# Delta-rule solver: inverses of the 16x16 diagonal blocks on VectorE, TensorE from size 16 on, and the next key projection ahead of the solver

## What is computed

```python
    decay = jnp.exp(jnp.where(lower_incl, gcum[..., :, None] - gcum[..., None, :], -jnp.inf))
    kb = kc * bc[..., None]
    l_mat = jnp.where(strict, jnp.einsum('nbhid,nbhjd->nbhij', kb, kc) * decay, 0.0)
    rhs = jnp.concatenate([vc * bc[..., None], kb * jnp.exp(gcum)[..., None]], axis=-1)
    sol = lax.linalg.triangular_solve(l_mat, rhs, left_side=True, lower=True, unit_diagonal=True)
    ...
    def step(s, xs):
        q_d, k_d, u_c, w_c, a_c, d_c = xs
        v_new = u_c - jnp.einsum('bhcd,bhde->bhce', w_c, s)
        o = jnp.einsum('bhcd,bhde->bhce', q_d, s) + jnp.einsum('bhij,bhje->bhie', a_c, v_new)
        s = s * d_c[..., None, None] + jnp.einsum('bhcd,bhce->bhde', k_d, v_new)
        return s, o
```

## Time and profile before

| what | us |
|---|---|
| median of the three runs | 1915.28 |
| lowest and highest of them | 1913.55, 1915.35 |
| span of the profiled execution, first to last instruction | 1911.3 |
| total time of the profiled execution | not listed apart |
| PE, DVE, ACT, POOL busy in it | 1860.4, 1257.7, 976.3, 525.6 |
| delta stage, head 0 to the last product of head 7 | 809.0 to 1306 |

### The profile page before, as it was taken

One profiled execution on the slowest core, in us unless ns is written; L12 is line 12 of the kernel. 1 busy time (PEld: TensorE's weight loads), 2 busy tenths in 40 slices (PEclk: granted clock), 3 DMA queues, 4 the chain that ended last, 5 costly groups with the idle time before them and its releaser, 6 DMA issues.

```text
span 1911.3 us, 32275 instructions
## 1 busy us (share of the span) xinstructions
PE 1860.4 (97%) x11917; PEld 1737.8 (91%) x11917; DVE 1257.7 (66%) x2099; ACT 976.3 (51%) x1869; POOL 525.6 (28%) x398
## 2 busy tenths in 40 slices
PE   8899999999998999999999999999999999999997
PEld 5899999999997799999999999997888989899897
DVE  7758787778666765467666766676333577366476
ACT  6534242424457655557555755574223576365463
POOL 0714141323100200255355534550000034142330
PEclk9999999999999999999999999999999999999999
DMA  8143335553423420011101111111333403223232
GB/s 332 62 132 122 122 116 165 179 180 119 145 76 111 120 61 1 23 39 61 50 33 38 60 49 33 38 45 56 99 99 105 149 23 113 87 89 118 82 133 67
DMA packets 52241, 178.36 MB, mean 93 GB/s; under 512 B 6820, under 2 KB 10020, under 8 KB 51888
## 3 DMA queue, kind: packets, MB, share of 16 engines
q1 hardware_dynamic: 48864, 162.46, 25.1%
q0 software_dynamic: 3280, 14.60, 2.4%
HBM read 170.17 MB, written 4.24 MB: 91 GB/s over the span
## 4 chain that ended last, share of the span: by engine, by line
PE 75%; DVE 9%; ACT 8%; issue 5%; POOL 2%; DMA 1%; SPq 0%; ACTq 0%; DVEq 0%; POOLq 0%
PE ps L2621 50%; PE ps L2832 14%; PE ps L2625 4%; PE ps L2919 2%; PE ps L3152 1%; DMA raw<-W 1%; PE ps L3076 1%; ACT e_hi L1261 1%; DVE e_lo L2024 1%; ACT ps L1246 1%; DVE d_os L2515 1%; DVE d_c L2383 1%; PE ps L3106 1%; PE ps L3208 1%; DVE ps L2066 1%
## 5 line engine op out<-in xcount | busy, mean ns | idle before, releaser
L2621 PE MATMUL ps<-h_hi,w_hi 128*128 128x384 f32 (+2 forms) x720 | 241.1, 373 | 8.0 <-DVE h_lo L1800 4.0
L2621 PE MATMUL ps<-h_lo,w_hi 128*128 128x384 f32 (+2 forms) x720 | 236.9, 361 | 0.0
L2621 PE MATMUL ps<-h_hi,w_lo 128*128 128x384 f32 (+2 forms) x720 | 228.0, 356 | 0.0
L1730 DVE TENSOR_TENSOR w_lo<-raw,w_hi 128x1024 fp32r<-128x1024 f32 (+1 forms) x98 | 122.8, 1253 | 129.8 <-ACT w_hi L933 129.8
L933 ACT ACTIVATE w_hi<-raw 128x1024 fp32r<-128x1024 f32 (+1 forms) x98 | 102.9, 1050 | 153.9 <-PE ps L2621 151.9
L2621 PEld LDWEIGHTS ps<-h_hi,w_hi 128*128 128x128 f32 x720 | 130.1, 188 | 28.7 <-DVE h_lo L1800 8.2
L2621 PEld LDWEIGHTS ps<-h_hi,w_lo 128*128 128x128 f32 x720 | 133.0, 188 | 13.5
L2621 PEld LDWEIGHTS ps<-h_lo,w_hi 128*128 128x128 f32 x720 | 133.1, 188 | 13.0 <-issue 1.2
L2621 PE MATMUL ps<-g_hi,w_hi 128*128 128x384 f32 (+2 forms) x444 | 132.9, 346 | 0.8 <-DVE w_lo L1730 0.5
L2621 PE MATMUL ps<-g_lo,w_hi 128*128 128x384 f32 (+2 forms) x444 | 131.8, 343 | 0.0
L2621 PE MATMUL ps<-g_hi,w_lo 128*128 128x384 f32 (+2 forms) x444 | 131.7, 343 | 0.0
(11 more groups left out here) (465 smaller groups left out, 5459.7 us busy)
## 6 DMA issues: line engine op xcount, KB each, us to landing
raw<-W SPq DMA_DIRECT2D x221, 512.0 KB, 3.6
w_mod<-WMOD SPq DMA_DIRECT2D x68, 512.0 KB, 3.8
g_row<-g_rows POOLq DMA_DIRECT2D x8, 768.0 KB, 4.5
X<-XT SPq DMA_DIRECT2D x4, 768.0 KB, 6.9
a_sw<-i_n POOLq DMA_DIRECT2D x40, 64.0 KB, 1.9
w_first<-WMOD SPq DMA_DIRECT2D x4, 512.0 KB, 10.9
X<-XT SPq DMA_DIRECT2D x1, 2048.0 KB, 14.0
x_spill<-X POOLq DMA_DIRECT2D x1, 2048.0 KB, 9.5
```

Of the source, the lines that this page charges most:

```text
L1730: v.tensor_tensor(lo, src, hi.bitcast(F32), ALU.subtract).then_inc(s("w_split"), 1)
L2621: return pe.matmul(out, lhsT, rhs, start=start, stop=stop)
```

## The change

The solver's first four levels (sizes 1 to 8) are replaced. DVE's six products now carry the minus sign and a reciprocal of its own (`k_neg`), SP writes the six matrices to DRAM and reads the 48 diagonal 16x16 blocks back so that each lies in one partition (`d_b`, with a row of padding per matrix that makes the stride regular). DVE inverts all 48 at once, in place, in 14 steps of two products and two sums on up to 56 elements (`inverse_step`). SP returns the blocks in six small DMAs (`d_xc`), and DVE spreads each over its row of blocks with a mask (`own_block`). PE goes on from size 16: 9 groups and three levels. The key projection of the next head stands ahead of the solver (45 of its 48 pieces), the value projection fills the scan; the norm of a head's output moves to the top of the next head. POOL's list is in another order, and the pairs of semaphores in the attention that told of a step and its successor are one each. In the last head the second gate projection of the merge stands ahead of the solver.

```diff
-LEVELS = 7
+SUB = 16
+NB = P // SUB
+LV0, LEVELS = 4, 7
...
+            def blocks_out(h):
+
+                sp.wait_ge(s("d_l"), h + 1)
+                sp.dma_start(DL[:, 0:P].rearrange("c p j -> p c j"), d_l[:, 0]).then_inc(s("d_blocks"), 16)
+                sp.wait_ge(s("d_blocks"), h * 32 + 16)
+                sp.dma_start(d_b[0:NB * NCH], diagonal).then_inc(s("d_blocks"), 16)
+
+            def blocks_back(h):
+
+                sp.wait_ge(s("inv_a"), 28 * h + 28)
+                for c in range(NCH):
+                    sp.dma_start(d_xc[:, c], d_b[NB * c:NB * c + NB]).then_inc(s(f"d_xin{c // 2}"), 16)
+
+            load_groups(B_LAST1 + 2 * RING, W_HEAD)
+            with sp.Fori(0, H, 1) as h:
+                blocks_out(h)
+                load(h * 4 + W_HEAD, W_HEAD % RING)
+                load(h * 4 + (W_HEAD + 1), (W_HEAD + 1) % RING)
+                blocks_back(h)
+                load(h * 4 + (W_HEAD + 2), (W_HEAD + 2) % RING)
+                load(h * 4 + (W_HEAD + 3), (W_HEAD + 3) % RING)
...
-                g.wait_ge(s("t_first"), h * 3 + 3)
-                for lv in (1, 2):
-                    for gr in range(3):
-                        level(lv, 2 * gr, 2 * gr + 2)
...
+                g.wait_ge(s("d_l"), h + 1)
+                level(LV0)
+                level(LV0 + 1)
+                next_low(5)
+                if not first:
+                    g.wait_ge(s("od_ss"), h)
+                g.wait_ge(s("d_tokc"), h * 2 + 1)
+                g.wait_ge(s("hc"), h * 2 + 2)
                 keys(0)
                 keys(1)
-                g.wait_ge(s("lvl"), h * 10 + 10)
+                if not final:
+                    g.wait_ge(s("d_diff"), h * 2 + 2)
+                    g.wait_ge(s("d_qe"), h * 2 + 2)
+                    rows_load(h + 1)
+                queries(0)
+                queries(1)
+                if not final:
+                    spread(h + 1)
+                g.wait_ge(s("sv_q"), h * 9 + 3)
+                level(LV0 + 2)
...
+                if not first:
+                    out_add(h - 1)
+                split_next(b[4])
+                if not first:
+                    out_low(h - 1)
+                    out_gain(h - 1)
+
+                m = d_b[0:NCH * NB]
+
+                def inverse_step(n):
+
+                    f, r = n + 1, SUB - 2 - n
+                    low = (m[:, f + 1:, f:f + 1], m[:, f:f + 1, 0:f], m[:, f + 1:, 0:f])
+                    up = (m[:, 0:r, r:r + 1], m[:, r:r + 1, r + 1:], m[:, 0:r, r + 1:])
+                    sums = [d_bt[0:NCH * NB, k, 0:f * r].rearrange("p (i j) -> p i j", i=r) for k in range(2)]
+                    for k, (col, row, rest) in enumerate((low, up)):
+                        if n:
+                            v.wait_ge(s("inv_a"), h * 28 + (2 * n - 1 + k))
+                        v.tensor_tensor(sums[k], col.to_broadcast([NCH * NB, r, f]), row.to_broadcast([NCH * NB, r, f]), ALU.mult)\
+                         .then_inc(s("inv_m"), 1)
+                    for k, (col, row, rest) in enumerate((low, up)):
+                        v.wait_ge(s("inv_m"), h * 29 + (2 * n + 2 + k))
+                        v.tensor_tensor(rest, rest, sums[k], ALU.add).then_inc(s("inv_a"), 1)
+
+                v.wait_ge(s("d_blocks"), h * 32 + 32)
+                v.memset(m.rearrange("p i j -> p (i j)")[:, 0:SUB * SUB:SUB + 1], 1.0).then_inc(s("inv_m"), 1)
+                for n in range(SUB - 2):
+                    inverse_step(n)
...
+                if not final:
...
+                    conv(h + 1, 0, b[4])
+                if not first:
+                    out_rows(h - 1)
+                split_next(b[6])
+
+                for gr in range(3):
+                    v.wait_ge(s(f"d_xin{gr}"), h * 32 + 32)
+                    x = d_x[:, 2 * gr:2 * gr + 2].rearrange("p c (b j) -> p c b j", b=NB)
...
+                if final:
+                    query(b[5], 0, KT - 1)
+                else:
+                    piece(b[5], next_key, 6 * KT - 3)
...
-                for i in range(18):
+                for i in range(9):
                     mid(i)
                     if i:
                         grow(i - 1)
```

More of the change, by code:

```diff
@@ L1635, in _ @@
             take(first[1])
-            activate(0, first[1].ahead(2), False)
-            take(Blk(B_DN, 0, 2))
-            with a.Fori(0, H - 1, 1) as h:
-                dn_head(h, False)
-            dn_head(H - 1, True)
+            a.preload_act_table_set(SILU_SET)
+            split(first[1].ahead(2))
+            key_silu(0)
+            dn_head(0, True, False)
+            with a.Fori(1, H - 1, 1) as h:
+                dn_head(h, False, False)
+            dn_head(H - 1, False, True)
             def merged(it):
@@ L3113, in dn_head @@
                 last.then_inc(s("d_kk"), 1)
+                pe.wait_ge(psum_read[b[2].pair], b[2].turn + 2)
+                tokens(0)
+                if not first:
+                    pe.wait_ge(s("od_copy"), h)
+                pe.wait_ge(s("d_silu"), h * 3 + 2)
                 for c in range(NC_X):
@@ L3117, in dn_head @@
                 last.then_inc(s("d_kq"), 1)
[L3118 to L3119 removed]
                 dn_gemm(h, 3)
[L3121 to L3124 removed]
+                query(b[4], 0, 2)
+                if not first:
+                    pe.wait_ge(s("d_tokc"), h * 2 + 1)
+                    out_sum(h - 1)
+                query(b[4], 2, 5)
                 pe.wait_ge(psum_read[b[3].pair], b[3].turn + 2)
@@ L3258, in _, with attended @@
             dn_gemm(0, 2)
-            with pe.Fori(0, H - 1, 1) as h:
-                dn_head(h, False)
-            dn_head(H - 1, True)
-            for j in range(2, 4):
-                merge_gemm(0, j)
+            dn_head(0, True, False)
+            with pe.Fori(1, H - 1, 1) as h:
+                dn_head(h, False, False)
+            dn_head(H - 1, False, True)
+            def attended(k0, k1):
+                blk = Blk(B_MERGE, 0, 2)
+                if k0 == 0:
+                    pe.wait_ge(s("w_split"), blk.w + 1)
+                    pe.wait_ge(psum_read[blk.pair], blk.turn + 1)
+                for k in range(k0, k1):
+                    pe.wait_ge(s("o_split"), k + 1)
+                    for i, (w, x) in enumerate(((w_hi, oat_hi), (w_hi, oat_lo), (w_lo, oat_hi))):
+                        last = mm(bank(blk, 1), w[:, blk.pair, k, :], x[:, k], k == 0 and i == 0, k == KT - 1 and i == 2)
+                if k1 == KT:
+                    last.then_inc(s("gemm_done"), 1)
+            attended(0, 3)
+            out_sum(H - 1)
+            attended(3, KT)
+            merge_gemm(0, 3)
             def merge(it):
```

562 lines of the change are left out of this document (276 added, 286 removed).

## The result

The changed kernel takes **1978.06 us**, the median of four runs (1976.01 to 1979.21), against 1914.41 for the kernel before on the same chip: a ratio of 1.0332, 95% interval 1.0317 to 1.0346. It is slower by 3.3%. The forecast was 1966, with 1885 to 1992 around it.

The account below looks back on a forecast made before the run. PE's work was taken to bound a head; after the change 53.3 us busy plus 17.2 idle made 70.5. Six middle heads at +7 (42) and two end heads at +4 each, together +50 on 1915.28, gave 1966 us, range 1885 to 1992.

Parts of the forecast that it names:

- The deciding term: DVE's all-SBUF inverse takes turns with POOL's queued instructions; it ends at 32.5 us, so PE idles 11.3 us per head.
- the undisturbed walk: Path to the start matrix without POOL's hold-ups: inverse ends at 19.6 us, blocks return in 4.3, matrix at about 23.9.
- DVE's share between two POOL instructions: In each gap between two POOL instructions the inverse gets one or two instructions, 0.8 us in all.
- The blocks: Diagonal blocks written to DRAM in 3.6 us and read back in 3.0, there at 12.6 us into a head.
- PE's idle time ahead of the start matrix: PE arrives at 25.3 us, waits until 36.6 and idles 11.3; 10 to 12 us would show the forecast right.
- the cover: PE's work in a head before its first wait for the solver's start matrix, 22.9 us.
- PE's work in a head: Nine full solver groups of 1.11 us go, 10.0 us, so PE's work falls from 63.3 to 53.3 us.
- The ends: Head 0, without a forerunner's output, and the last head, with nothing filling its scan, cost about +4 us each.
- Rival 1: DVE's inverse isn't held up by POOL: 57 us per head, 1870 us in all; chance 0.20.
- The break-even: Delay of DVE's inverse at which the change neither gains nor loses: 6.6 us, against the 13 expected.
- Rival 2: The inverse ends early, so the spread pair falls behind it: 64.6 us per head, 1922 us; chance 0.10.
- Rival 3: The DRAM path is the bound, 10 us not 6.6: 73 to 75 us per head, some 1990; chance 0.07.

Follow-up runs that it names:

- e1: Changed kernel with POOL's spread pair for the next head moved behind the solver's last mask; 1940.13 us, one run.
- e2: Changed kernel with POOL's key scaling, query scaling and spread pair, and DVE's next-query convolution, moved behind the solver; 1939.98 us, ratio 1.014.
- e3: Changed kernel with the inverse in a free PSUM bank, one input of each product and sum in PSUM, POOL unchanged; 1934.64 us, ratio 1.0103.
- e5: Changed kernel with the edits of e3 and e1 together, the spread pair behind the value scaling; 1890.89 us, ratio 0.987.
- e7: e5 with POOL's first two masks moved behind its query scalings; 1904.44 us, ratio 0.9945.
- e9: Changed kernel with unused PE products (8, 44 and 4) filling PE's three gaps in a head; 1969.55 us, ratio 1.0294.
- e8: e5 with POOL's first masks after the output's gain, row load behind query scalings, value weight split behind the solver's first masks; 1885.47 us, ratio 0.9857.

## Why the prediction was right, and where it was off

**The deciding term held.** The prediction put the inverse's end at 32.5 us and the start matrix at 36.6; they came at 31.6 and 36.1. It had the inverse held up by 12.9 us (19.6 to 32.5); the rows give 12.8. It expected about ten held instructions; there are six, in five pairs. Undisturbed it takes 6.6 us (forecast 7.0), and from its end to the start matrix go 4.5 us (forecast 4.1, where the undisturbed walk has 4.3). e1, e2, e3 and e5 show the cause: move POOL's work or one operand, and the delay goes. Four things stand beside it:

- **DVE's share between two POOL instructions** was taken as one or two instructions a gap, 0.8 us in all. From 1036.0 to 1044.0 DVE got three pairs through in eight microseconds of POOL's work, so the size holds. That the two "strictly take turns" does not: a product was held for 2.67 us over both query scalings, and one in e7 for 4.44 us. Why POOL kept its turn there and not at the key scalings, no run tells. The spread pair still met the inverse, with 2.6 us of undisturbed steps left (forecast 3.2).
- **The blocks** were to be there at 12.6 and were used at 12.1, but this hides two errors. The path through DRAM was sized by the 512 KB loads and a guess, 6.6 us; it took 2.8 us for the write and 2.1 for the read, 4.9, so the blocks lay there at 10.8. DVE came for them only at 12.1, since its two instructions ahead were held by the masks (1.93 and 2.32 us; 0.69 and 0.74 in e7). The estimate of 5.0 us from the Trainium skill ("DMA: Bandwidth & Descriptors", "Anatomy of one DMA"), which the sum did not take, agrees with the 4.9 measured, though the page gives its fit for DMAs issued by GpSimd and these go by SP's queue. The DMA rows:

```profile
d_matrices<-d_l SPq DMA_DIRECT2D x8, 384.0 KB, 2.8
d_xc<-d_b SPq DMA_DIRECT2D x48, 8.0 KB
d_b<-d_matrices SPq DMA_DIRECT2D x8, 48.0 KB, 2.1
```

- **PE's idle time ahead of the start matrix** is 10.3 us in heads 4 to 6, where PE comes at 25.8 (forecast 11.3 and 25.3; the cover is 0.7 us longer than 22.9). In head 3 it is 8.7, outside the 10 to 12 that was to be the sign, because the low clock in the key projection (0.84 us a pair for 0.51) lets PE come 1.6 us later, at 27.4. An idle time is a difference of two arrivals: the matrix came at 36.1 in both, and the head didn't get longer.
- **PE's work in a head** was to be 53.3 us. With the clock up it is 55.0 (e5). The nine full groups went as forecast: from its first product to its last the solver takes 10.6 us in e5 and took 20.5 before. Of the 1.7 us above the forecast 0.7 lies in the cover and the rest behind it. In head 4 of the changed kernel it is 57.4, 2.4 more at the low clock, and in head 3, with the low clock in the key projection, 59.0.

There is luck in the head's 70.5, then. Its busy part was 4.1 us too small (57.4 in head 4 for 53.3) and its idle part 3.1 too large (14.1 for 17.2: 2.2, 10.3, 0.7 and 0.9 for 2.4, 11.3, 2.0 and 1.5), and the two nearly cancel.

**Where the size was off** is the total: +50 us against +63.7. The middle heads were 6 x 7 = 42 and are 6 x 8.0 = 48. What the sum has no term for is the granted clock after the wait: 1.6 us per head, for with the clock up the head takes 70.0 (e9), half a microsecond less than forecast. Behind the start matrix the head took 35.4 us where the forecast had 33.9, and 33.8 with the clock up. The ends were to cost 4 + 4. Head 0 takes 69.9 us where it took 63.1, and head 7 with the step to the merge 64.0 where it took 57.7: 6.8 + 6.3, and some 2 behind them. These two were not walked as the middle head was, and more than half of the missing 13.7 lies there and behind them. No run takes it apart further.

**The rivals.** Rival 1, an inverse that isn't held up, was priced at 57 us per head and 1870 us in all. e3 made exactly that, and the head is 66.7 and the kernel 1934.64. Its price was too low by 65 us, mostly because the walk let DVE's work behind the inverse run undisturbed: 7.7 of the 8.0 us by which the start matrix is late (31.9 for 23.9). In the changed kernel it does, since POOL is through by then; take the inverse out of the way and it meets the same POOL instructions. The break-even given for it (6.6 us of delay) is wrong for the same reason. Rival 2, the spread pair behind the inverse, was priced at 64.6 and 1922; e1 gives 65.9 and 1940. Rival 3, the path through DRAM, is off the critical chain by 1.3 us in a middle head, where DVE never idled for the memset; only in head 0, which has no output norm ahead of it, did it idle 4.2 us.

**What stays open.** Why the clock fell in the key projection in heads 1 to 3 of the changed kernel and not in heads 4 to 6 or in e5, with the same wait of 1.8 us ahead of it, no run tells. Whether more can be had from e8 by a faster return of the blocks wasn't tried.

## What to carry to other kernels

Before a chain of small DVE instructions is put beside POOL's work, look at their operands: with all of them in SBUF each can cost a whole POOL instruction or more, however few elements it has, and a chain of dependent ones pays it each time. One operand in PSUM frees the chain (here 19.4 us became 7.5 for the same work). Then walk every SBUF instruction of DVE up to the one that others wait for against POOL's queue, for a collision that is removed moves to the next of them: only the two edits together made the change a gain, from 1978 to 1891 us with 1915 before.

## What the runs showed of the hardware

- Few elements don't help beside POOL: two products of 12 elements took 2.48 us beside two query scalings (e3), 4.52 beside a query scaling and two masks (e7), and 0.24 alone.
- DVE and POOL don't always alternate: of each of these pairs one product was held over all of POOL's instructions (2.40 and 4.44 us) and the other took under 0.2.
- A DVE instruction with one SBUF tensor and a scalar is held as well: the first tap of a convolution over 770 elements takes 0.62 us at the start of a head and 2.30 beside POOL's mask in the scan of e3:

```profile
1055.85 2.30 DVE L2425 TENSOR_SCALAR d_kc<-d_up,hn 128x770 f32<-128x770 f32 x1
```

- PE's granted clock was 0.50 behind an idle time of 8.6 us and came back some 7 us after PE had begun again. Short waits don't always bring it down: in e8 it was low behind 0.24, 0.84 and 0.90 us in head 3 and stayed up behind 0.23, 1.02 and 0.90 in head 5.
- SP takes 3.91 us to issue the six DMAs that spread 8 partitions over 128, 0.6 us each, where 0.4 had been assumed and the write of the six matrices takes 0.40:

```profile
1028.01 0.40 SPq L728 DMA_DIRECT2D d_matrices<-d_l  x1
...
1053.62 3.91 SPq L736 DMA_DIRECT2D d_xc<-d_b  x6
```
